# Block sums of a feed-forward's last product on GpSimd: operands asked for early, weight sums one pass ahead, entry work reordered

## The reference

```python
D_MODEL, FFN_DIM = 1024, 2816

def swiglu_half(x, pre, post, w_gate, w_up, w_down):
    h = rmsnorm(x, pre)
    y = (jax.nn.silu(h @ w_gate) * (h @ w_up)) @ w_down
    return x + 0.5 * rmsnorm(y, post)

def layer(...):
    h = swiglu_half(x, W['ffn1_pre'], W['ffn1_post'], W['ffn1_gate'], W['ffn1_up'], W['ffn1_down'])
    ...                                   # three branches, merged, times w_out
    h = h + rmsnorm(merged @ W['w_out'], W['mix_post'])
    y = swiglu_half(h, W['ffn2_pre'], W['ffn2_post'], W['ffn2_gate'], W['ffn2_up'], W['ffn2_down'])
```

## Time and profile before

| what | us |
|---|---|
| median of the timed runs | 3238.22 |
| their range (3 runs) | 3233.7 to 3240.38 |
| the profiled execution's own time | 3234.39 |
| its span | 3232.6 |

### The profile page before, as it was taken

How to read it: one execution, slowest core, us unless ns; L and a number is a source line. 1 busy time by engine, 2 the same in 40 slices (tenths; PEclk the granted TensorE clock), 3 DMA queues, 4 the chain that set the end, 5 groups by cost and what they waited for, 6 DMA issues and landing times. The chain is left out here.

```text
span 3232.6 us, 65488 instructions
## 1 busy us (share of the span) xinstructions
PE 2958.6 (92%) x27498; PEld 2796.9 (87%) x27498; DVE 1790.0 (55%) x2864; ACT 1132.5 (35%) x2182; POOL 792.4 (25%) x884
## 2 busy tenths in 40 slices
PE   8999994799999988979999989999998999994798
PEld 8999994799899988838777579999998999994798
DVE  7777662447544646667554542444427776762455
ACT  5333331334111323244665351212234333331334
POOL 3444444104000213330003000000034444444103
PEclk9999997899999999988999999999998999997899
DMA  5555555654522220011016631112213555555654
GB/s 169 172 168 176 174 179 172 195 171 147 150 89 75 61 87 4 18 23 49 11 45 193 229 130 48 50 50 53 68 58 98 171 171 173 170 188 167 210 179 133
DMA packets 417278, 393.89 MB, mean 122 GB/s; under 512 B 50616, under 2 KB 368353, under 8 KB 416218
## 3 DMA queue, kind: packets, MB, share of 16 engines
q1 hardware_dynamic: 383962, 277.57, 28.8%
q0 software_dynamic: 31984, 112.13, 10.2%
q10 hardware_dynamic: 1040, 0.00, 0.0%
HBM read 284.11 MB, written 105.53 MB: 121 GB/s over the span
## 5 line engine op out<-in xcount | busy, mean ns | idle before, releaser
L2129 PE MATMUL banks<-hid_pieces,dn_high 128*128 128x258 f32 x2464 | 458.4, 289 | 135.6 <-DVE hid_pieces L2071 128.9
L2129 PEld LDWEIGHTS banks<-hid_pieces,dn_high 128*128 128x128 f32 x2464 | 389.8, 194 | 137.7 <-DVE hid_pieces L2071 128.7
L1893 PE MATMUL banks<-x_pieces,gate_pieces 128*128 128x258 f32 x3360 | 414.8, 283 | 0.3 <-DVE sq L1986 0.2
L1893 PE MATMUL banks<-x_pieces,up_pieces 128*128 128x258 f32 x3360 | 414.5, 283 | 0.1
L1893 PEld LDWEIGHTS banks<-x_pieces,gate_pieces 128*128 128x128 f32 x3360 | 408.7, 189 | 0.7 <-DVE sq L1986 0.7
L1893 PEld LDWEIGHTS banks<-x_pieces,up_pieces 128*128 128x128 f32 x3360 | 408.6, 189 | 0.4 <-DVE sq L1986 0.3
L2129 PE MATMUL banks<-hid_pieces,dn_part 128*128 128x258 f32 x1232 | 351.8, 286 | 0.0
L1167 PEld LDWEIGHTS banks<-XG,pR 128*128 128x128 f32 (+1 forms) x1800 | 283.2, 187 | 10.3 <-issue 6.1
L1167 PE MATMUL banks<-XG,pR 128*128 128x344 f32 (+1 forms) x1800 | 288.7, 321 | 3.7 <-DVE pR L2664 2.9
L1167 PE MATMUL banks<-XR,mg_gate 128*128 128x344 f32 x1728 | 283.3, 319 | 1.3 <-PEq L53 1.3
L1167 PEld LDWEIGHTS banks<-XR,mg_gate 128*128 128x128 f32 x1728 | 273.8, 188 | 1.6 <-issue 1.6
(11 more groups left out here) (552 smaller groups left out, 5427.1 us busy)
## 6 DMA issues: line engine op xcount, KB each, us to landing
hid_spill<-h_stage SPq DMA_DIRECT2D x44, 516.0 KB, 3.7
chain_slot<-hid_spill POOLq DMA_DIRECT2D x66, 258.0 KB, 3.5
t_sums<-chain_slot POOLq DMA_DIRECT2D x66, 258.0 KB, 2.4
chain_slot<-in_ffn_down POOLq DMA_DIRECT2D x66, 256.0 KB, 3.7
w_sums<-chain_slot POOLq DMA_DIRECT2D x66, 256.0 KB, 2.4
dn_low<-w_sums SPq DMA_DIRECT2D x32, 384.0 KB, 3.6
praw<-in_w_in SPq DMA_DIRECT2D x24, 512.0 KB, 4.2
sq<-in_w_in SPq DMA_DIRECT2D x24, 512.0 KB, 4.1
```

Of the source, the lines that this page charges most:

```text
L1893: ins = k.nc.tensor.matmul(out, self.w[m][:, a, w, f * P:(f + 1) * P], self.x[p][:, b, x, f * TQ:(f + 1) * TQ], start=first and f == 0 and ...
L2129: ins = k.nc.tensor.matmul(k.ps[2 * j + q][:, 0:TQ], a[s][:, f * P:(f + 1) * P], k.hid_pieces[m % 2][:, q, f, b, :], start=m in self.FRESH ...
```

## The change

Four things are changed in the class and in its two uses.

1. The chain (`chain_loads`, `chain_slots`, `chain_parts`, `chain`). The slots y and z change places from one block to the next. A block's fourth operand goes into y, the slot of its first sum, as soon as that sum's store has landed, and it is asked for ahead of the third sum's store. A load for the next block waits for one store only, that of its own slot (four semaphores `chain_stored` in place of two), and a sum waits for its own operands (four semaphores `chain_landed` in place of one). The order of the blocks becomes S0, S1, T0, S2, T1, ... S10, T9, T10, so that a weight sum is made a pass before it was.
2. The store of the last pass's first half moves ahead of two loads on SyncE.
3. In the last problem the splits for unit 0 stand earlier: `first_down_high` ahead of the copy of product 6 on ScalarE; `hidden_low(0, 0)`, `hidden_low(0, 1)` and `first_down_low` earlier on VectorE.
4. At the end, `add_up` and `spread` of groups 0 and 1, their `root` and `inverse`, and the norms of group 1 stand half a unit to two units later.

```diff
@@ SyncE: sp_passes, sp_down_ahead, sp_down
             if it + 1 < self.N:
                 self.load_gate(sp, it + 1)
+                self.store_hidden(sp, it, 0)
             else:
                 self.sp_down_ahead(sp)
-            self.store_hidden(sp, it, 0)
...
         for i in range(2):
             self.load_hidden(sp, 0, i)
+        self.store_hidden(sp, it, 0)
         self.product[4].wait(sp, self.last - 4)
         self.load_hidden(sp, 0, 3)
         self.load_down(sp, 1)
...
-        self.chain_sums.wait(sp, 2 * self.CHAIN)
+        self.chain_sums.wait(sp, 4 * self.CHAIN)
+        self.chain_stored[2].wait(sp, self.CHAIN)
         self.load_hidden(sp, 1, 4)
@@ GpSimd: the chain
-    CHAIN = 4 * (FT // 2)
+    CHAIN = 2 * (FT // 2)
+    CHAINS = [("S", 0)] + [x for i in range(FT // 2) for x in [("S", i + 1)] * (i + 1 < FT // 2) + [("T", i)]]
...
+    def chain_loads(self, pool, n):
+        kind, i = self.CHAINS[n]
+        if kind == "T":
+            self.hid_stored.wait(pool, 2 * i + 2)
+        slots, parts = self.chain_slots(n), self.chain_parts(n)
+        for r, stored in enumerate((1, 2, 3)):
+            self.chain_stored[stored].wait(pool, n)
+            self.chain_landed[r].done(pool.dma_start(slots[r], parts[r]))
+
+    def chain_slots(self, n):
+        x, y, z = (0, 1, 2) if n % 2 else (0, 2, 1)
+        return [self.k.chain_slots[r][:, 0:4 * P if self.CHAINS[n][0] == "S" else 2 * TQ] for r in (x, y, z)]
...
-        for t in self.chain_stored:
-            t.wait(pool, t.n)
-        for dst, a in zip((x, y, z), src):
-            self.chain_landed.done(pool.dma_start(dst, a))
-        self.chain_landed.wait(pool, self.chain_landed.n)
+        landed[0].wait(pool, n + 1)
+        landed[1].wait(pool, n + 1)
         s.done(nc.gpsimd.tensor_tensor(y, x, y, ALU.add if kind == "S" else ALU.subtract))
         s.wait(pool, at + 1)
-        yz.done(pool.dma_start(out[:, 0, :], y))
+        stored[0].done(pool.dma_start(out[:, 0, :], y))
+        landed[2].wait(pool, n + 1)
         s.done(nc.gpsimd.tensor_tensor(x, z, x, ALU.subtract))
         s.wait(pool, at + 2)
-        xs.done(pool.dma_start(out[:, 2, :], x))
...
+        stored[1].done(pool.dma_start(out[:, 2, :], x))
+        a, b = (y, z) if kind == "S" else (z, y)
+        s.done(nc.gpsimd.tensor_tensor(z, a, b, ALU.subtract))
         s.wait(pool, at + 3)
-        yz.done(pool.dma_start(out[:, 1, :], z))
-        xs.wait(pool, xs.n)
-        self.chain_landed.done(pool.dma_start(x, src[3]))
-        self.chain_landed.wait(pool, self.chain_landed.n)
-        s.done(nc.gpsimd.tensor_tensor(x, x, z, ALU.subtract))
+        stored[0].wait(pool, n + 1)
+        landed[3].done(pool.dma_start(y, self.chain_parts(n)[3]))
+        stored[2].done(pool.dma_start(out[:, 1, :], z))
+        landed[3].wait(pool, n + 1)
+        s.done(nc.gpsimd.tensor_tensor(y, y, z, ALU.subtract))
         s.wait(pool, at + 4)
-        xs.done(pool.dma_start(out[:, 3, :], x))
+        stored[3].done(pool.dma_start(out[:, 3, :], y))
@@ ScalarE: problem_act
+        if n == self.last:
+            self.first_down_high(act)
         self.copy(act, n, 6)
...
@@ VectorE: problem_dve
+        if n == self.last:
+            self.hidden_low(dve, 0, 0)
         if n > 4:
             self.combine(dve, n - 1, 21)
...
+        if n == self.last:
+            self.hidden_low(dve, 0, 1)
         self.total(dve, n, 11)
         if n == self.last:
-            for i in range(2):
-                self.hidden_low(dve, 0, i)
+            self.first_down_low(dve)
@@ the ends of both FFNs (the second's lines name fin for mid)
-                      lambda g: (6, 2, 2)[g], lambda g: (7, 0, 3)[g], 2.0, ffn1.SQUARES, {0: (0, 7), 1: (2, 0), 2: (2, 3)},
+                      lambda g: (6, 2, 2)[g], lambda g: (7, 0, 3)[g], 2.0, ffn1.SQUARES, {0: (2, 4), 1: (2, 1), 2: (2, 3)},
...
-                if (u, q) in ((20, 0), (28, 1)):
-                    post.add_up(pe, u // 28)
                 if (u, q) in ((20, 1), (29, 1)):
-                    post.spread(pe, u // 29)
+                    post.add_up(pe, u // 29)
+                if (u, q) in ((21, 0), (30, 1)):
+                    post.spread(pe, u // 30)
...
-                if u in (20, 29):
-                    post.root(act, u // 29)
+                if u in (21, 30):
+                    post.root(act, u // 30)
...
-                if u == 31:
-                    mid.high(act, 1, range(0, 4))
...
-            mid.high(act, 1, range(4, DT))
+            mid.high(act, 1)
...
-                if u in (20, 29):
-                    post.inverse(dve, u // 29)
-                if u in (21, 22, 30, 31):
-                    g = u // 30
-                    for f in (range(0, 4 + g) if u in (21, 30) else range(4 + g, DT)):
+                if u in (21, 30):
+                    post.inverse(dve, u // 30)
+                if u in (21, 22, 31):
+                    g = u // 31
+                    for f in {21: range(0, 4), 22: range(4, DT), 31: range(0, DT)}[u]:
                         mid.norm(dve, g, f)
```

More of the change, by code:

```diff
@@ L1711, in chain @@
[L1711 to L1718 removed]
+        parts = {"S": [(even, high), (odd, high), (even, low), (odd, low)], "T": [(even, two), (even, one), (odd, two), (odd, one)]}
@@ L1719, in chain @@
+        whole = self.dn_src if kind == "S" else self.k.hid_spill
+        return [whole[:, f, c] for f, c in parts[kind]]
+    def chain(self, pool, n):
+        k, nc = self.k, self.k.nc
+        kind, i = self.CHAINS[n]
+        x, y, z = self.chain_slots(n)
+        s, stored, landed, at = self.chain_sums, self.chain_stored, self.chain_landed, 4 * n
+        out = (k.w_sums if kind == "S" else k.t_sums)[:, :, i, :]
+        landed[0].wait(pool, n + 1)
+        landed[1].wait(pool, n + 1)
         s.done(nc.gpsimd.tensor_tensor(y, x, y, ALU.add if kind == "S" else ALU.subtract))
@@ L1745, in norm_x @@
+        for n in range(len(self.CHAINS)):
+            self.chain_loads(pool, n)
+            self.chain(pool, n)
     def norm_x(self, dve, p, fs):
@@ L3946, in between @@
             def between(act, u):
-                if u in (20, 29):
-                    fin.post.root(act, u // 29)
+                if u in (21, 30):
+                    fin.post.root(act, u // 30)
             def squared(act, g, f):
```

46 lines of the change are left out of this document (15 added, 31 removed).

## The result

The changed kernel takes 3133.82 us (median of 4 runs, 3126.61 to 3137.01), the kernel before 3237.99 us over the 4 runs timed beside it (3233.7 to 3240.38). The ratio is 0.9677, 95% interval 0.9657 to 0.9696. The forecast was 3131, range 3106 to 3162. The profiled execution took 3137.01 us (span 3135.0), the slowest of its four, while the one of before lay 3.6 us under its median; so the spans of the two traces differ by 97.6 us and the medians by 104.2.

What follows compares the result with a forecast made beforehand. The prediction took GpSimd's slow chain, seen as TensorE's 59.98 and 64.07 us gaps, as the bound. 117.7 - 4.9 - 6.0 = 106.8 us off 3234.4 gives 3127.6, plus 3.8 for the median: 3131 us, range 3106 to 3162.

Steps and rivals of the forecast that it cites:

- The bound and the pace: GpSimd's chain causes both gaps at unit 4; a block falls from 23.2 to 18.1 us computed, 19 taken.
- the rival that the prediction built on it: Chain on GpSimd: no overlap worth the name, blocks stay near 23 us, total 3225 to 3240 us; chance 0.04.
- The point of decision: Chain on GpSimd: any pace below 19.9 us a block lets T10 start when its data lands.
- It is why the order matters as much as the overlap.: Chain order: S10 no longer between T9 and T10; at 19 us the chain has only about 18 us of slack.
- T10 and what is behind it: Last store to TensorE resuming at unit 4: 6.2 + 19 + 9.4 us; both FFNs together gain 117.7 us.
- The entry: Start of the down product: earlier split, store and load give back 4.4 us in each FFN.
- Clock behind the gap: TensorE behind unit 4's gap: nothing credited for the clock; 3 us in each FFN left to the range.
- Sums and end: Group 0's sums lose 4.9 us net, spread waits 4.9 and 5.4 us; the later end loses 6.0 us.
- The slower rival: Passes: denser GpSimd additions and DMAs slow VectorE or weights; at 2 us a problem, 3291 us; chance 0.03.
- The sum: Whole kernel: 117.7 - 4.9 - 6.0 = 106.8 us gained, forecast median 3131 us.

Runs made afterwards that it cites:

- e11: Changed kernel with the fourth operand's load late, as in the kernel before, the first three still early: 3144.78 us, ratio 0.9752.
- e2: Changed kernel, but each block asks for its first three operands only when all four stores of the block before have landed: 3165.44 us, ratio 0.9771.
- e3: Kernel before with the new block order alone, loads and stores as before: 3239.66 us, ratio 1.001.
- e1: Changed kernel with the blocks in their old order (S0, T0, S1, T1, ...): 3135.84 us, ratio 0.968.
- e5: Changed kernel with the entry's old order (last pass's first store, splits on ScalarE and VectorE): 3136.68 us, ratio 0.969.
- e6: Changed kernel with a place of its own for T10's third slot, so hidden part 4's load need not wait for T10: 3111.52 us, ratio 0.9612.
- e7: Changed kernel with group 0's root and inverse ahead of unit 21's splits, group 1 timed as in the kernel before: 3105.5 us, ratio 0.9594.
- e4: Changed kernel with the sums of squares, root, inverse and norms timed as in the kernel before: 3119.75 us, ratio 0.9632.

## Why the prediction was right, point by point

**The bound and the pace.** Right. Both gaps came from the chain; a block went from 23.2 to 19.0 and 18.5 us (forecast 18.1 computed, 19 taken). Its parts were sized less well: the fourth operand's early load brings 1.0 to 1.8 us in a block, where I gave it 0.5 to 1 in T10 (e11), and the early requests 2.2 to 2.7 us (e2's 21.2 against 18.5 to 19.0), not 3.1. Slower transfers are a likely reason for the difference: the median 256 KB load of the chain now lands in 4.4 us for 3.7. The Trainium skill (DMA: Bandwidth & Descriptors, Issuing engines are not separate DMA queues) says that DMAs of all issuing engines run on the same 16 DMA engines and interleave. The trace agrees in direction, with these 0.7 us; the rival that the prediction built on it did not come true, since the overlap still won. The 2.67 us that the prediction set beside the page's figure for 258 KB is GpSimd's idle time behind the issue; from issue to landing that load took 3.1 us.

**The point of decision.** Right: 19.9 us was worked out, and T10 can start 422.1 and 422.6 us after S0, which is 20.1 us a block. At 20.2 and 20.5 us (e11) the change loses 11 us of its gain, at 21.2 (e2) 32 us, and near 23 T10 comes as late as before (e3).

**"It is why the order matters as much as the overlap."** Wrong. The step took 21 blocks ahead of T10 for a merit of the new order, but there are 21 in either. In the old order T10 would be late only if T9 and S10 took more than the 52.5 us between the landings that T9 and T10 wait for (447.84 and 500.30 in e1), that is above 26 us a block, where 21 blocks are later still. e1 and e3 show no effect at either pace.

**T10 and what is behind it.** Taken as 6.2 + 19 + 9.4 us; measured 6.8 + 17.7 + 10.0 in the first FFN and 6.1 + 18.5 + 10.1 in the second (494.10, 500.90, 518.57, 528.52; 2872.64, 2878.78, 2897.29, 2907.37). TensorE resumed at 528.52 where 529.0 was forecast. In the second FFN 2951.3 was forecast; less the 49.5 us by which its chain began earlier this is 2901.8, and it was 2907.37. The last store was the late part, 5.4 us: 2.5 by slower passes, 2.3 by a smaller gain at the entry, the rest not placed.

**The entry.** The mis-sized term: 8.8 us forecast, 2 to 3 measured (e5). The wait for unit 0's weight split went, as forecast (3.01 and 3.57 us before), but the wait for part 2 that I let stand at 1.7 us grew to 4.02 and 4.15 (1.22 and 2.51 before). TensorE's idle time at the entry so fell by 0.2 and 1.9 us only. Part 2's load went out 8.4 us earlier in the first FFN (478.85 for 487.28), but beside larger ones issued just ahead of it, and took 6.9 us to land for 3.4. The clock is at half behind the wait.

**Clock behind the gap.** As taken, nearly nothing gained. TensorE runs at half clock for 5.7 and 5.9 us behind the gaps of 5.32 and 6.71 us, and did so for 7.8 and 7.5 us behind those of 59.98 and 64.07; that is some 2 us less at half clock, 1 us of time, in each FFN. Window of the changed kernel, columns as above, of which the first 2.4 us are the end of the gap:

```profile
2905.00:2910.00 5.00, 2.08 (x8) 1.81 (x9) 3.90 (x4) 5.00 (x8) 0.00 (x0) 0.50 1.11 327
```

e6, where the gap is gone, gives 8.7 and 10.2 us in U for waits of 5.9 and 7.3 us: the rest, 2.8 and 2.9 us, is the clock.

**Sums and end.** The waits at the spread were forecast at 4.9 and 5.4 us and came at 5.30 and 6.27, through the root's place on ScalarE as described; e7 proves the mechanism by removing it. Net 3.9 us lost for 4.9 forecast. The end cost 2.5 + 5.9 = 8.4 us for 6.0. VectorE's last norms and addition in the second FFN, which answer to the earlier trace rows:

```profile
3104.47 0.57 DVE L3752 SCALAR_TENSOR_TENSOR tiles<-tiles,vec,banks 128x344 f32<-128x344 f32 x1 [0.24 <-PE banks L1339]
...
3111.63 0.41 DVE L2195 TENSOR_TENSOR tiles<-tiles,banks 128x258 f32<-128x258 f32 x1
```

The addition starts 3.5 us after the start of the product's last matmul (3108.12), where it had been 0.4 us (3211.75 before): 3.1 us later for the 4.0 worked out. What I left out is the clock: the wait at the last `add_up` grew by the same 3.1 us, from 0.56 to 3.65, and 6.8 us of F2 are at half clock, none before.

**The slower rival** was right in kind and wrong in size: the passes did meet later weights (8.6 us for 7.0), but only the second FFN's lost, 2.5 us over some 40 problems, far from 1.3 us each.

**The sum.** 106.8 forecast. The stretches give 113.5 in U (gap and clock) and 1.4 in E where 117.7 was forecast, 12.3 for 10.9 lost in sums and end, 2.5 in the second passes; that makes 100.1, and start, P1 and M bring it to 97.7. The medians, free of the accident of one execution, say 104.2. So the main term was right to 3 us in 118, and the rest is three small costs set too low and a gain at the entry set too high.

## What to carry to other kernels

Before you make a side chain faster, work out the time at which its consumer can start at best: a pace faster than that is worth nothing, and a pace just slower counts once for every block (here the point is 20.1 us a block, with 21 blocks). Ask what exactly the last wait is for. Here it was the place of a buffer, and moving it took 22 us off that no faster pace of the blocks ahead could give; yet it buys only the length of one block where the chain itself is late. And look at what an order of instructions puts behind a load that has not landed: a root of 0.26 us behind four splits cost more than 5 us twice.

## What the runs showed of the hardware

- The same block T10 takes 14.4 and 14.5 us when nothing else moves (129 and 128 GB/s in all, e2), 17.7 and 18.5 us beside the entry's loads (241 and 237 GB/s), and 21.2 and 20.1 us beside the next units' loads too (280 and 286 GB/s, e6). How long a chain of transfers takes depends on what moves beside it.
- Starting earlier can make a transfer chain longer: of the 23.2 us by which e2's T10 starts late, 3.3 us come back.
- The same code with the same waits can get different clocks: the stretch F1 was at half clock for 27 us in e4's trace and for 14 us in e7's and in that of before, 108.5 us for 102.7 and 103.1. What decides it is not shown.
- A stretch of 16,000 matmuls with the same code took from 1660.9 to 1669.3 us in thirteen kernels. A difference of some us between two single traces has to be placed before it is believed.
